# Issuing the compressed-branch transposes of the next head one unit earlier on TensorE

## The chip, the core and the metric

The kernel runs on one core of a Trainium2 chip. A core has engines that run their own instruction streams and meet through semaphores: TensorE (PE: matmuls, and PEld for its weight loads), VectorE (DVE), ScalarE (ACT), GpSimd (POOL), and SyncE (SP), which here only starts DMA transfers. The metric is the device time of the one launch, in microseconds; lower is better. The part that matters here is attention, where three engines pass small tiles to each other unit by unit.

## The reference

One decoder layer on 512 tokens of width 1024, in float32: an adaptive norm, a combined input projection, two groups of attention heads, an output projection, and a grouped mixture of 16 experts. The part around the change is the first head group, which has three branches over the same queries:

```
q_n = rms_norm(q_n, q_gain_n) * ATTN_SCALE
o_cmp, p_cmp = nsa_compressed(q_n, k_c, v_c, ...)     # 31 compressed keys, each from 32 tokens
o_slc = nsa_selected(q_n, k_sl, v_sl, p_cmp, ...)     # 8 blocks, all selected at this length
o_win = banded_attention(q_n, k_w, v_w, ..., 512)
o_nsa = g0 * o_cmp + g1 * o_slc + g2 * o_win
# nsa_compressed:
s = q @ kc.T - slope * dist;  s = where(valid, s, -1e30)
p = softmax(s) * row_valid;   o = p @ vc
```

The second group (SWA) is banded attention with window 128 and a learned sink per head.

## The kernel before

Heads are worked on in pairs, one head of each of the two key/value groups on 64 partitions each. There are GQ = 4 pairs t = 0 to 3 of the first group (NSA) and 4 of the second. A pair of the first group is cut into NU = 5 units j = 0 to 4, a pair of the second into 2; u counts all 28 units. Every unit goes through the same steps, and each engine has its own order, written out by hand:

- TensorE `scores(u)` (L1366): queries times keys into one of two pairs of PSUM banks (score).
- VectorE `masked(u)` (L969): adds the position term, takes the row extreme, writes `probs`; three buffers.
- ScalarE `exps(u)` (L585): exponentials with their sums.
- VectorE `weights(u)` (L989, L996, L1001): multiplies by gate over sum.
- TensorE `weighed_T(u)` (L1379): transposes the weighted probabilities, eight 128x128 tiles.
- ScalarE and VectorE `evac(u)` (L596, L1009): each copies one half to SBUF.
- TensorE `values(u)` (L1402): product with V, accumulated in PSUM over the five units of the pair. For j = 0 the accumulation starts with L1392, the product of the compressed branch, which needs `pcT`.

The compressed branch of pair t runs beside them: `cmp_scores` on TensorE (L1411), `cmp_masked` on VectorE (L1016 to L1018), `cmp_exp` on ScalarE (L601), `cmp_weights` on VectorE (L1022, L1023, L1025, L1026), which signals `c_w`; then `cmp_T` on TensorE (L1418), four transposes that wait for `c_w` and signal `c_t`; then `cmp_T` on ScalarE (L606), a copy to `pcT` that signals `c_T`. ScalarE runs its copy behind `out_T` of the pair before (L576, L577). VectorE makes the scores and weights of pair t + 1 in units 3 and 4 of pair t: in unit 4 in the order masked(u + 2), evac(u), weights(u + 1), cmp_weights(t + 1). TensorE is three units ahead with its scores: in unit u it issues scores(u + 3), which is the last thing it does in the unit.

A wait stops the whole instruction stream of its engine: what stands behind a waiting instruction on TensorE doesn't start. Four more pieces touch the order: `queries_T` (L1354), the transposed queries of the next pair, in unit 1; the preamble with scores(0) to scores(2) and cmp_T(0); and behind attention the output projection (L1454), the routing and the experts (L1524 to L1549). SyncE loads expert weights 0 when the last `values` is through (`a_pv`). The lines of the loop that the change touches:

```
                if 0 < t < GQ and j == 0:
                    cmp_T(t)
                if t < GQ - 1 and j == 1:
                    queries_T(t + 1)
```

Of the kernel before, what the change touches and what calls it, by code (L numbers as in the profile page):

```python
# [19 lines left out]
GQ = HN // KV  # L20
# [32 lines left out]
def decoder_layer(nc, x, c, w_router, ada_w, ada_b, norm1_g, norm2_g, w_in, w_out, nsa_q_gain, nsa_k_gain,  # L53
# [6 lines left out]
    with ctx:  # L60
# [283 lines left out]
        def unit_of(u):  # L344
            if u < GQ * NU:
                return u // NU, u % NU, NSA_UNITS[u % NU]
            i, j = (u - GQ * NU) // SU, (u - GQ * NU) % SU
            return GQ + i, j, SWA_UNITS[j]
# [4 lines left out]
        def slot_of(t):  # L353
            return t % 2 if t < GQ else SWA_SLOT[t - GQ]
# [438 lines left out]
        def _(dve):  # L793
# [107 lines left out]
            for n, (c0, r0, _) in enumerate(KSRC):  # L901
                nc.vector.tensor_tensor(khat[:, n, :, :].rearrange("p i (v d) -> p i v d", v=KV),
                                        proj[:, :, c0:c0 + KV * DH].rearrange("p i (v d) -> p i v d", v=KV),
                                        hrstd[:, :, r0:r0 + KV].unsqueeze(3).broadcast_to([P, TT, KV, DH]), ALU.mult).then_inc(s_khat, 1)
# [316 lines left out]
        def _(pe):  # L1221
# [124 lines left out]
            def queries_T(t):  # L1346
                pe.wait_ge(a_q, t + 1)
                Y = banks[6 + (t if t < GQ else GQ) % 2]
                if t > GQ:
                    pe.wait_ge(a_qT, t)  # L1350
                if GQ >= t >= 2:
                    pe.wait_ge(n_o, t - 1)
                for i in range(TT):
                    m = nc.tensor.transpose(Y[:, i * P:(i + 1) * P], qhat[t % 2][:, i, :], ident[:])  # L1354
                m.then_inc(a_qt, 1)

            def scores(u):
                t, j, segs = unit_of(u)
                if j == 0:
                    pe.wait_ge(a_qT, t + 1)  # L1360
                if u >= 2:
                    pe.wait_ge(a_m, u - 1)
                for q, r, off, w, k0 in segs:
                    for b in range(2):
                        half = slice(b * DH, (b + 1) * DH)
                        m = nc.tensor.matmul(banks[2 * (u % 2) + b][:, off:off + w], qT[half, slot_of(t), q * P:(q + 1) * P],  # L1366
                                             kT[half, r, k0:k0 + w], start=True, stop=True)
                m.then_inc(a_s, 1)

            def weighed_T(u):  # L1370
                t, j, segs = unit_of(u)
                pe.wait_ge(a_d, u + 1)
                if u >= 1:
                    pe.wait_ge(a_ev_a, u)
                    pe.wait_ge(a_ev_v, u)
                for q, r, off, w, k0 in segs:
                    for at0 in range(off, off + w, P):
                        for b in range(2):
                            m = nc.tensor.transpose(banks[4 + b][:, at0:at0 + P], probs[:, u % 3, b, at0:at0 + P], ident[:])  # L1379
                m.then_inc(a_t, 1)  # L1380

            def values(u):
                t, j, segs = unit_of(u)
                O = banks[6 + t % 2]
                if j == 0:
                    if t >= 2:
                        pe.wait_ge(n_o, min(t - 1, GQ))
                    if t > GQ + 1:
                        pe.wait_ge(w_o, t - GQ - 1)
                    if t < GQ:  # L1390
                        pe.wait_ge(c_T, t + 1)
                        nc.tensor.matmul(O, vcBD[0:2 * NK, :], pcT[0:2 * NK, :], start=True, stop=False, skip_group_check=True)  # L1392
                    else:
                        if t == GQ:
                            pe.wait_ge(a_qT, 2 * GQ)
                        nc.tensor.matmul(O, zeros_b[:, 0:P], zeros_b[:], start=True, stop=False, skip_group_check=True)
                pe.wait_ge(a_ev_a, u + 1)
                pe.wait_ge(a_ev_v, u + 1)
                for q, r, off, w, k0 in segs:
                    for n in range(w // P):  # L1400
                        for b in range(2):
                            m = nc.tensor.matmul(O[b * DH:(b + 1) * DH, q * P:(q + 1) * P],  # L1402
                                                 proj[:, k0 // P + n, V_COL[r] + b * DH:V_COL[r] + (b + 1) * DH],
                                                 probsT[:, u % 2, b, off + n * P:off + (n + 1) * P], start=False, stop=False,
                                                 skip_group_check=True)
                m.then_inc(a_pv, 1)

            def cmp_scores(t):
                pe.wait_ge(a_qT, t + 1)
                for i in range(TT):  # L1410
                    m = nc.tensor.matmul(banks[6 + t % 2][:, i * 2 * NK:(i + 1) * 2 * NK], qT[:, slot_of(t), i * P:(i + 1) * P], kcBD,  # L1411
                                         start=True, stop=True)
                m.then_inc(c_s, 1)

            def cmp_T(t):
                pe.wait_ge(c_w, t + 1)
                for i in range(TT):
                    m = nc.tensor.matmul(banks[6 + t % 2][0:2 * NK, i * P:(i + 1) * P], scm[:, i, :, :].rearrange("p b n -> p (b n)"),  # L1418
                                         ident[:], start=True, stop=True)
                m.then_inc(c_t, 1)  # L1420
# [8 lines left out]
            for u in range(N_UNITS):  # L1429
                t, j, segs = unit_of(u)  # L1430
                weighed_T(u)
                if u >= 1:
                    values(u - 1)
                if 0 < t < GQ and j == 0:
                    cmp_T(t)
                if t < GQ - 1 and j == 1:
                    queries_T(t + 1)
                if t == GQ - 1 and j >= 1:
                    queries_T(GQ + j - 1)
                if t < GQ - 1 and j == 2:  # L1440
                    cmp_scores(t + 1)
                if u + 3 < N_UNITS:
                    scores(u + 3)
            values(N_UNITS - 1)
# [157 lines left out]
```

## Time and profile before

| what | us |
| --- | --- |
| median of 3 runs | 766.3 (763.06 to 767.3) |
| profiled execution | 763.06 |
| its span | 761.3 |
| TensorE busy | 619.2 (81%) |
| VectorE busy | 325.2 (43%) |
| ScalarE busy | 253.6 (33%) |

A busy time says how long an engine had work in it, not whether that work set the end. Attention lies between about 197 and 324 us of the span; for a change there the timelines of the engines side by side say more than the shares of the whole span. An idle time with a releaser (`<-DVE pool_sb L1001`) says that the engine stood still until that instruction was done. In the profile `score` and `bank` are PSUM tiles; `pool_sb` is a large SBUF tile that holds, among much else, `probs`, `probsT`, `scm` and `pcT`.

### The profile page before, as it was taken

Reading aid. Unit: us, or ns where it says so; the run is one execution under the profiler, and the core shown is the slowest. Engines: PE = TensorE matmul, PEld = TensorE weight load, DVE = VectorE, ACT = ScalarE, POOL = GpSimd, SP = SyncE. Lnnn points to the kernel's source line nnn. Section 1 sums busy time; section 2 is a strip of 40 time slices with the busy share of each in tenths; the row PEclk is TensorE's granted clock in tenths of the full one; section 3 lists DMA queues with packets and bytes.
Section 4 is the critical chain, followed back from the end, with each engine's and each line's share of the span. In section 5 each row is a group of like instructions: output and inputs, shape, how many; then the busy total and the mean of one; then the engine's idle time right before and its main releaser. Section 6 shows DMA issues by size and latency. Waiting matters only on the chain.

```text
span 761.3 us, 15584 instructions
## 1 busy us (share of the span) xinstructions
PE 619.2 (81%) x6207; PEld 371.4 (49%) x6211; DVE 325.2 (43%) x925; ACT 253.6 (33%) x611; POOL 78.2 (10%) x118
## 2 busy tenths in 40 slices
PE   0898999967599998799972288989999999999940
PEld 0544474654366666554462154545555555555520
DVE  3714828242578999822445021222222222222215
ACT  4200200132357668711230142434433433443410
POOL 5001000034100000000001200101001101100122
PEclk9998999989689999999965599999999999999985
DMA  8970957070799000092081659999999999999228
GB/s 323 379 299 10 404 194 274 2 232 0 234 302 250 17 2 1 1 335 107 0 320 46 218 174 352 362 360 363 369 360 361 370 362 362 363 374 355 59 53 309
DMA packets 81388, 176.25 MB, mean 231 GB/s; under 512 B 9410, under 2 KB 26378, under 8 KB 79306
## 3 DMA queue, kind: packets, MB, share of 16 engines
q1 hardware_dynamic: 68592, 152.90, 57.5%
q0 software_dynamic: 8384, 13.97, 5.4%
q10 hardware_dynamic: 4380, 8.94, 3.7%
q8 instruction: 21, 0.34, 0.2%
q14 instruction: 11, 0.09, 0.0%
HBM read 155.02 MB, written 20.71 MB: 231 GB/s over the span
## 4 chain that ended last, share of the span: by engine, by line
PE 27%; DMA 23%; DVE 2%; issue 2%; POOL 2%; ACTq 0%; ACT 0%; POOLq 0%
DMA featT<-expert_rows 21%; PE score L1534 9%; PE score L1454 7%; PE score L1543 4%; PE bank L1524 4%; PE score L1494 2%; DMA pool_sb<-expert_rows,idx 1%; POOL expert_rows L768 1%; POOL pool_sb L788 1%; DMA expert_rows<-pool_sb,idx 1%; DMA expert_rows<-featT 1%; PE bank L1549 0%; ACTq L664 0%; PE bank L1486 0%; PE bank L1402 0%
## 5 line engine op out<-in xcount | busy, mean ns | idle before, releaser
L1534 PE MATMUL score<-pool_sb,featT 128*32 128x256 f32 x2688 | 161.4, 384 | 23.4 <-DMA featT<-expert_rows 14.7
L1534 PEld LDWEIGHTS score<-pool_sb,featT 128*32 128x32 f32 x2688 | 86.4, 110 | 84.4 <-DMA featT<-expert_rows 29.9
L1250 PE MATMUL bank<-pool_sb,featT 128*128 128x512 f32 (+2 forms) x256 | 89.3, 511 | 5.8 <-DVE featT L843 2.6
L1190 DVE TENSOR_TENSOR featT<-featT,score 128x128 f32<-128x128 f32 x42 | 12.1, 288 | 186.2 <-ACT featT L675 186.2
L1543 PE MATMUL score<-pool_sb,featT 128*32 128x256 f32 x1344 | 82.8, 387 | 0.4 <-ACT featT L680 0.4
L1250 PEld LDWEIGHTS bank<-pool_sb,featT 128*128 128x128 f32 x256 | 50.0, 196 | 43.5 <-issue 35.8
L669 ACT ACTIVATE featT<-bank,mod_col 128x32 f32<-128x32 f32 x129 | 39.3, 374 | 61.5 <-PE bank L1524 61.5
L776 POOL DMA_DIRECT2D expert_rows<-featT x42 | 29.1, 692 | 280.2 <-DVE featT L1186 266.5
L1180 DVE TENSOR_SCALAR featT<-bank,mod_col 128x32 f32<-128x32 f32 x215 | 51.0, 303 | 15.1 <-PE bank L1524 15.1
L1454 PE MATMUL score<-pool_sb,featT 128*128 128x512 f32 x128 | 55.6, 594 | 0.0
L675 ACT ACT_TABLE_LOAD x42 | 53.9, 1283 | 0.8
L1543 PEld LDWEIGHTS score<-pool_sb,featT 128*32 128x32 f32 x1344 | 39.9, 111 | 24.7 <-issue 1.4
L585 ACT ACTIVATE pool_sb<-pool_sb,nmax 128x128 f32<-128x128 f32 (+2 forms) x96 | 50.0, 526 | 4.5 <-DVE nmax L969 4.5
L675 ACT ACTIVATE featT<-score 128x128 f32<-128x128 f32 x42 | 11.6, 277 | 116.1 <-PE score L1534 116.1
L1524 PE MATMUL bank<-ident,featT 32*128 32x32 f32 x344 | 29.8, 226 | 19.6 <-DMA featT<-expert_rows 19.6
L1524 PEld LDWEIGHTS bank<-ident,featT 32*128 32x128 f32 x344 | 25.0, 139 | 37.0 <-DMA featT<-expert_rows 19.7
L1379 PE MATMUL bank<-ident,pool_sb 128*128 128x128 f32 x216 | 30.7, 286 | 14.2 <-DVE pool_sb L1001 14.0
L859 DVE SCALAR_TENSOR_TENSOR pool_sb<-pool_sb,cond 128x2048 f32<-128x2048 f32 x16 | 37.6, 2347 | 3.6 <-DMA pool_sb<-in_ada_w 2.6
L1454 PEld LDWEIGHTS score<-pool_sb,featT 128*128 128x128 f32 x128 | 24.0, 190 | 29.4 <-issue 28.9
L1379 PEld LDWEIGHTS bank<-ident,pool_sb 128*128 128x128 f32 x216 | 23.9, 144 | 29.1 <-DVE pool_sb L1001 27.4
L1366 PE MATMUL score<-pool_sb 64*128 64x256 f32 (+3 forms) x192 | 34.3, 475 | 0.9 <-ACT pool_sb L570 0.9
L1186 DVE TENSOR_TENSOR featT<-score,gate_part 128x256 f32<-128x256 f32 x42 | 17.8, 425 | 34.0 <-PE score L1543 34.0
(243 smaller groups left out, 688.0 us busy)
## 6 DMA issues: line engine op xcount, KB each, us to landing
pool_sb<-in_moe_w SPq DMA_DIRECT2D x48, 2048.0 KB, 21.2
pool_sb<-in_ada_w SPq DMA_DIRECT2D x16, 1024.0 KB, 7.4
expert_rows<-zeros_f SPq DMA_DIRECT2D x17, 512.0 KB, 6.2
featT<-expert_rows ACTq DMA_DIRECT2D x44, 128.0 KB, 5.5
expert_rows<-featT POOLq DMA_DIRECT2D x42, 128.0 KB, 7.1
pool_sb<-in_ada_w SPq DMA_DIRECT2D x8, 640.0 KB, 12.3
pool_sb<-in_w_out SPq DMA_DIRECT2D x4, 1024.0 KB, 16.7
pool_sb<-in_ada_w SPq DMA_DIRECT2D x8, 384.0 KB, 9.7
```

The costliest lines, as they stand in the source:

```text
L585: m = nc.scalar.activation(p, p, ACT.Exp, scale=-1.0, bias=nmax[:, u % 3, b, n:n + 1], accum_out=sums[:, u % 3, b, n:n + 1])
L669: m = nc.scalar.activation(xgT[:, 5 + k, :], banks[5][:, k * BT:(k + 1) * BT], ACT.Identity, scale=mod_col[:, 21 + k:22 + k], bias=mod_col ...
L675: nc.scalar.activation(silu, banks[0][:, 0:HB], ACT.Silu).then_inc(m_si, 1)
L859: nc.vector.scalar_tensor_tensor(out=acc[:, g % 2, :], in0=stage[:, n % 3, :], scalar=cond[:, k:k + 1], in1=acc[:, g % 2, :], op0=ALU.mult ...
L1180: m = nc.vector.tensor_scalar(xgT[:, k, :], banks[4][:, k * BT:(k + 1) * BT], mod_col[:, 16 + k:17 + k], mod_col[:, 24 + k:25 + k], ALU.mu ...
L1250: m = nc.tensor.matmul(pj_bank(g, i)[:, 0:n], featT[:, k, i * P:(i + 1) * P], w_stage[:, g % 3, k, 0:n], start=(k == 0), stop=(k == KD - 1))
L1366: m = nc.tensor.matmul(banks[2 * (u % 2) + b][:, off:off + w], qT[half, slot_of(t), q * P:(q + 1) * P], kT[half, r, k0:k0 + w], start=True ...
L1379: m = nc.tensor.transpose(banks[4 + b][:, at0:at0 + P], probs[:, u % 3, b, at0:at0 + P], ident[:])
L1454: m = nc.tensor.matmul(banks[2 * (j % 2) + g], featT[:, 4 * g + k, i * P:(i + 1) * P], w_out_sb[:, 4 * g + k, h], start=(k == 0), stop=(k ...
L1524: m = nc.tensor.transpose(banks[4 + k // 5][:, at0:at0 + BT], xg[:, k * P:(k + 1) * P], ident[0:BT, 0:BT])
L1534: mm = nc.tensor.matmul(banks[0][h * BT:(h + 1) * BT, 0:2 * HB], xgT[:, k, :], exp_w13[slot][:, :, k, h * HB:(h + 1) * HB], start=(k == 0) ...
L1543: mm = nc.tensor.matmul(banks[2][h * BT:(h + 1) * BT, 0:DN], hT[:, c * BT:(c + 1) * BT], exp_w2[slot][:, c, h * DN:(h + 1) * DN], start=(c ...
```

## The change

In the unit loop of TensorE the call of `cmp_T` for pair t leaves unit 0 of pair t, where it stood behind values(u - 1), and is made in unit 4 of pair t - 1, again behind values(u - 1) and ahead of scores(u + 3). This holds for pairs 1, 2 and 3; cmp_T(0) in the preamble stays where it is. Nothing else is changed.

```
@@ -1431,14 +1431,14 @@
                 weighed_T(u)
                 if u >= 1:
                     values(u - 1)
-                if 0 < t < GQ and j == 0:
-                    cmp_T(t)
                 if t < GQ - 1 and j == 1:
                     queries_T(t + 1)
                 if t == GQ - 1 and j >= 1:
                     queries_T(GQ + j - 1)
                 if t < GQ - 1 and j == 2:
                     cmp_scores(t + 1)
+                if t < GQ - 1 and j == 4:
+                    cmp_T(t + 1)
                 if u + 3 < N_UNITS:
                     scores(u + 3)
```

The instructions of TensorE from the values product in unit 4 of pair 0 on; names in brackets are the semaphores that an instruction waits for (`a_m`: masked, `a_d`: weights, `a_ev_a` and `a_ev_v`: the copies, `c_w`: cmp_weights). A minus is the order before, a plus the order after:

```order
 L1402 MATMUL bank<-pool_sb 64x128 [waits a_ev_v,a_ev_a]
 L1402 MATMUL bank<-pool_sb 64x128 x7
-L1366 MATMUL score<-pool_sb 128x128 [waits a_m]
-L1366 MATMUL score<-pool_sb 128x128
-L1366 MATMUL score<-pool_sb 128x384 x2
-L1379 MATMUL bank<-ident,pool_sb 128x128 [waits a_ev_v,a_ev_a,a_d]
-L1379 MATMUL bank<-ident,pool_sb 128x128 x7
-L1402 MATMUL bank<-pool_sb 64x128 [waits a_ev_v,a_ev_a]
-L1402 MATMUL bank<-pool_sb 64x128 x7
 L1418 MATMUL bank<-ident,pool_sb 64x128 [waits c_w]
 L1418 MATMUL bank<-ident,pool_sb 64x128 x3
+L1366 MATMUL score<-pool_sb 128x128 [waits a_m]
```

The four transposes L1418, with their wait for `c_w`, now stand in front of a scores group, a group of probability transposes and a values group which they stood behind.

VectorE's stream at the same place, the end of unit 4 and the start of unit 0 of the next pair, is the same before and after:

```order
L1001 TENSOR_SCALAR pool_sb<-pool_sb,fac 128x512 [waits a_chain]
L1022 TENSOR_REDUCE cfac<-pool_sb 128x8 [waits c_e]
L1023 RECIPROCAL cfac<-cfac 128x8 [waits a_chain]
L1025 TENSOR_TENSOR cfac<-cfac,gates 128x8 [waits a_chain]
L1026 TENSOR_TENSOR pool_sb<-pool_sb,cfac 128x256 [waits a_chain]
L969 ISA pool_sb,nmax<-score,pool_sb 128x128 [waits a_t,a_s]
```

L1026 signals `c_w`; the masking L969 right behind it waits for `a_s`, the scores group L1366 that TensorE now issues behind L1418.

## Rows read from the trace of the kernel before

**Rows 1.** The page: TensorE's busy tenths in 40 slices of the span.

```profile
PE   0898999967599998799972288989999999999940
```

**Rows 2.** One period; columns: length, busy PE, PEld, DVE, ACT, POOL, clock, DMA.

```profile
235.76:256.90 21.14, 19.31 (x175) 13.44 (x175) 19.12 (x72) 14.35 (x44) 0.00 (x0) 1.00 0.60 165
```

**Rows 3.** Waits of attention, 197 to 325 us: total, times, longest.

```profile
PE bank L1379 <- DVE pool_sb L1001: 14.0, 18, 1.6
DVE pool_sb L969 <- PE score L1366: 9.1, 8, 4.2
```

**Rows 4.** TensorE's timeline: start, length, instruction, idle time before it.

```profile
250.25 1.14 PE L1366 MATMUL score<-pool_sb 64*128 64x128 f32 x8
252.46 1.09 PE L1379 MATMUL bank<-ident,pool_sb 128*128 128x128 f32 x8 [1.07 <-DVE pool_sb L1001]
253.48 1.09 PE L1402 MATMUL bank<-pool_sb 128*64 128x128 f32 x16
254.40 1.04 PE L1418 MATMUL bank<-ident,pool_sb 128*64 128x128 f32 x8
255.37 1.14 PE L1366 MATMUL score<-pool_sb 64*128 64x128 f32 x8
256.90 1.09 PE L1379 MATMUL bank<-ident,pool_sb 128*128 128x128 f32 x8 [0.39 <-DVE pool_sb L1001]
...
260.58 1.13 PE L1366 MATMUL score<-pool_sb 64*128 64x256 f32 x8
```

**Rows 5.** VectorE: all four L1026, then its timeline at the same boundary.

```profile
L1026 DVE TENSOR_TENSOR pool_sb<-pool_sb,cfac x4: 424/425/426, 208.3 to 274.4; 128x256 f32<-128x256 f32 x4
...
253.21 0.43 DVE L1026 TENSOR_TENSOR pool_sb<-pool_sb,cfac 128x256 f32<-128x256 f32 x1
253.55 0.28 DVE L969 CUSTOM_DVE_ANT_0 pool_sb<-score,pool_sb 128x128 f32<-128x128 f32 x1
...
254.97 0.69 DVE L1009 COPY pool_sb<-bank 128x512 f32<-128x512 f32 x1
...
259.34 0.17 DVE L989 RECIPROCAL fac<-sums 128x4 f32<-128x4 f32 x1
...
261.77 0.42 DVE L969 CUSTOM_DVE_ANT_0 pool_sb<-score,pool_sb 128x256 f32<-128x256 f32 x1 [0.89 <-PE score L1366]
```

**Rows 6.** ScalarE's timeline at the same boundary.

```profile
253.59 0.60 ACT L596 ACTIVATE pool_sb<-bank 128x512 f32<-128x512 f32 x1 [1.42 <-PE bank L1379]
254.62 0.60 ACT L576 ACTIVATE pool_sb<-bank 128x512 f32<-128x512 f32 x1 [0.44 <-PE bank L1402]
...
258.13 0.58 ACT L596 ACTIVATE pool_sb<-bank 128x512 f32<-128x512 f32 x1
```

**Rows 7.** TensorE's timeline in the first pair, at the slower granted clock.

```profile
208.77 1.97 PE L1418 MATMUL bank<-ident,pool_sb 128*64 128x128 f32 x8 [2.12 <-DVE pool_sb L1026]
210.66 1.97 PE L1379 MATMUL bank<-ident,pool_sb 128*128 128x128 f32 x8
212.56 2.08 PE L1366 MATMUL score<-pool_sb 64*128 64x128 f32 x8
```

**Rows 8.** TensorE's timeline: instructions behind three longer idle times.

```profile
175.58 14.03 PE L1325 MATMUL bank<-pool_sb 128*62 128x256 f32 x64 [2.88 <-DVE pool_sb L914]
195.62 0.31 PE L1343 MATMUL bank<-ident,pool_sb 31*128 31x31 f32 x1 [3.47 <-DVE pool_sb L930]
459.56 0.64 PE L1534 MATMUL score<-pool_sb,featT 128*32 128x256 f32 x8 [1.60 <-DMA featT<-expert_rows]
```

**Rows 9.** Stretches behind these idle times, columns as in rows 2.

```profile
175.58:178.00 2.42, 2.42 (x11) 1.54 (x12) 0.00 (x0) 0.00 (x0) 2.42 (x1) 1.00 0.00 0
195.62:208.77 13.15, 9.09 (x30) 4.82 (x30) 7.38 (x22) 6.08 (x14) 0.72 (x2) 0.50 0.97 324
208.77:214.60 5.83, 5.83 (x24) 4.06 (x24) 3.18 (x14) 2.52 (x9) 0.00 (x0) 0.50 1.04 346
459.56:463.90 4.34, 4.34 (x48) 2.18 (x48) 1.47 (x6) 1.19 (x4) 0.00 (x0) 0.62 1.05 387
```

More of the change, by code:

```diff
@@ L1433, in _ @@
                     values(u - 1)
-                if 0 < t < GQ and j == 0:
-                    cmp_T(t)
                 if t < GQ - 1 and j == 1:
@@ L1441, in _ @@
                     cmp_scores(t + 1)
+                if t < GQ - 1 and j == 4:
+                    cmp_T(t + 1)
                 if u + 3 < N_UNITS:
```

## The prediction

> **What bounds the kernel now.** I read the page first, then the busy time of one period, the waits, and the timelines of TensorE, VectorE and ScalarE around one boundary between two heads. On the page TensorE has 81% of the span, but in the part that the change touches (about 197 to 323 us) it is not full everywhere: slices 12 to 17 of its row read 9, 9, 9, 9, 8, 7 [rows 1]. From one second unit of a head to the next, 21.14 us, TensorE is busy 19.31 and VectorE 19.12 [rows 2]. Neither alone is the bound. They hand over to each other: TensorE waits 14.0 us in 18 pieces for the weighted probabilities of VectorE (L1001), and VectorE waits 9.1 us in 8 pieces for scores of TensorE (L1366) [rows 3].
>
> Where in a head does which engine set the pace? Around the boundary into head pair 2, TensorE finishes the values product before 250.25, does the scores of the next unit 2 (250.25), then idles 1.07 us until VectorE releases the transposes of unit 0 at 252.46; then values, the moved transposes L1418 (254.40 to 255.37), scores of unit 3 (255.37), and again 0.39 us idle before unit 1 at 256.90 [rows 4]. VectorE is without a gap there: the last row of compressed weights (L1026) starts at 253.21 and the next masking of scores at 253.55 [rows 5]. So at the boundary VectorE is the bound and TensorE has slack. Behind unit 1 it is the other way round: VectorE idles 0.89 us before 261.77, waiting for the scores issued at 260.58 [rows 4, 5]. What lies behind attention starts from its last unit: output projection, routing, and the expert weights, whose loads SyncE holds until the last values product. I therefore count a delay inside attention in full at the end.
>
> **The change, part by part.** No instruction is added or removed. On TensorE the four transposes of cmp_T for heads 1, 2 and 3 go from unit 0 of their head to unit 4 of the head before: ahead of one scores group, one group of probability transposes and one values group. cmp_T(0) stays. The other queues are unchanged, and no DMA moves.
>
> *What it takes away:* four transposes between values and scores at unit 0, 255.37 - 254.40 = 0.97 us, three times [rows 4]. Worth nothing: there TensorE idles 0.39 us behind them already, released by VectorE. The earlier copy on ScalarE is worth nothing either: the product that needs it (L1392) is not waiting in the rows; it starts when the transposes ahead of it are through.
>
> *What it adds:* cmp_T waits for L1026, and now the scores of the next head's unit 2 are queued behind that wait. L1026 runs four times for 0.42 us [rows 5]. At this boundary it ends at 253.21 + 0.43 = 253.64; from the end of such a row to the first row on TensorE it takes 0.05 (208.3 + 0.42 = 208.72 against 208.77 [rows 5, 7]), so cmp_T starts at 253.69. Before it, TensorE is free from 250.25 on (less a few hundredths in which the values product ends): it now stands idle for 3.4 us in one piece. Then 0.97 for cmp_T: the scores start at 254.66 instead of 250.25. From the start of a scores group to VectorE's first masking it takes 261.77 - 260.58 = 1.19 us [rows 4, 5], so masking starts at 255.85 instead of 253.55: **2.3 us later**. This is the wait that replaces nothing: VectorE, the bound here, had its scores ready three microseconds early and now has none.
>
> Does it shorten again? VectorE runs masking, copy and weights without a gap from 253.55 until it releases unit 1 at 256.90, 3.35 us; after: 255.85 + 3.35 = 259.20, against 256.90, again 2.3. TensorE in that time does scores 1.06, transposes 1.02, values 1.0 and the scores of unit 3 (about 1.1) from 254.66: through at 258.84, in front of 259.20. The transposed probabilities of unit 0 reach VectorE at 255.72 + 1.13 = 256.85 (the 1.13 is 253.59 - 252.46 [rows 4, 6]), and VectorE wants them at 255.85 + 1.42 = 257.27 (1.42 is 254.97 - 253.55 [rows 5]); in time by 0.4. ScalarE comes closest: its block behind the values product took from 254.62 to the end of the exponentials at about 258.13 [rows 6], 3.5 us; the values product now ends so that the block starts at 255.72 + 1.02 + 1.14 = 257.88 (1.14 is 254.62 - 253.48 [rows 4, 6]), ending at 261.4, and VectorE wants the exponentials at 259.34 + 2.3 = 261.64 [rows 5]. In time by 0.2. From unit 1 on everything hangs on the released unit 1, the 0.89 us of VectorE included, because the scores that it waits for also come 2.3 us later. Nothing is given back. The same three boundaries: 3 x 2.3 = 6.9 us.
>
> *The clock.* The second term is the TensorE clock after the new gap. The period has a granted clock of 1.00, the 2.4 GHz level, with gaps of 1.07 us at most at its boundary [rows 2, 4]. A piece of 3.4 us is new here. The nearest rows on either side: behind a wait of 2.88 us at 175.58 the clock was 1.00; behind one of 3.47 us at 195.62 it was 0.50, the 1.2 GHz level, for 13 us and more [rows 8, 9]. Behind a short 1.60 us at 459.56, with small matmuls around it, it was 0.62 [rows 8, 9]. 3.4 is nearest to the one that fell. But the length of a gap does not decide alone, as the short one that fell and the longer one that held show, so I don't take all three: I take two of three.
>
> What does a slow resumption cost? Rows at the slow level: cmp_T 210.66 - 208.77 = 1.89 (0.97 fast), transposes 212.56 - 210.66 = 1.90 (1.02 fast), scores 214.60 - 212.56 = 2.04 (1.06 fast) [rows 7, 4]. Both groups that release VectorE are directly on the path: slow throughout, +0.92 and about +1.0. The next transposes add 0.88, of which 0.4 is covered. If the clock returns in the middle of the scores, the price is about 1.7; if it stays slow through values and the scores of unit 3 it is 1.9 + 0.5 + about 0.5 = 2.9; a clock that returns at once or is lost only late costs near 0. Upper bound: TensorE at half speed for the whole of the next packed stretch, as the 13 us of the first head, some 4.6. I take the middle of 1.7 and 2.9, **2.3 us for each slow resumption**; 2 x 2.3 = 4.6.
>
> The Trainium skill has a rule against this change: TensorE: Matmul & The Clock Gate, "HAM oscillation — how this bites in real kernels", says that idle waits between bursts of matmuls throttle the clock again, so that each burst starts cold. By that rule alone all three resumptions would be slow. The rows bear it out only in part: the 2.88 us wait kept its clock. The sum by the rule would be 3 x 2.3 + 3 x 2.3 = 13.8, by the row that held 6.9.
>
> **Sum.** 6.9 + 4.6 = 11.5 us. The profiled execution took 763.06 us (span 761.3 and 1.8 around it), the lowest of the three; it would become 774.6. The median of the runs is 766.3, and the forecast is made for the median: 766.3 + 11.5 = **777.8 us**.
>
> **Rivals.**
> 1. *The clock holds in all three gaps.* For it: 2.88 us kept it, and every gap in the heads so far. Against it: 3.47 us lost it. Time 766.3 + 6.9 = 773.2. Chance 0.16.
> 2. *All three resume slow* (what the skill's rule would give, here worked out from the rows above): 6.9 + 3 x 2.3 = 13.8, 780.1; with 2.9 each 781.9. For it: three gaps of equal length. Against it: the kept 2.88 us. With the forecast it is one family (at least one slow resumption), 0.70 together, of which 0.25 is this one.
> 3. *The delay is absorbed.* VectorE has 0.89 us of idle time behind unit 1 and a shorter one behind unit 2; if both soaked up the delay, 2.3 - 1.5 = 0.8 per boundary would be left, 2.4 in all: 768.7, which is within 0.5%. Against it: those idle times wait for TensorE, whose chain starts from the same late unit 1. Chance 0.06.
> 4. *Slow for long:* three resumptions at 4.6 and the 6.9: 766.3 + 20.7 = 787.0. For it: the first head, slow although TensorE was full from 208.77 to 214.60 [rows 7, 9]. Chance 0.06.
> 5. *Faster.* If L1026 were done before TensorE reaches cmp_T at 250.3, the moved transposes would fill idle time and unit 0 would be shorter by 0.97: at best 3 x 0.97 = 2.9 us, 763.4. The point from which it decides is VectorE 3.4 us earlier than the rows show; the price of VectorE's own work would have to drop for that. With TensorE clearly bound at the boundary it would be real. Chance 0.02; a gain under 3.8 us would then count as no change.
>
> **How the numbers follow.** The range has to hold 8 in 10. Low end: rival 1 less 1.5 for spread between runs (they lie 763.06 to 767.3): 771.5. High end: rival 2 with its higher price, 781.9, and 2.6 for the same spread and for a longer slow stretch: 784.5. Left out are rivals 3, 4, 5 and a little of each edge. A measurement of this kernel can tell about 0.5%, 3.8 us, from no change: 6.9 alone is beyond that. Slower: 0.70 + 0.16 + 0.06 = 0.92. Same: 0.07 (rival 3 and most of 5). Faster by more than that: 0.01.
>
> **What would show it.** In the changed profile TensorE's row at L1418 must carry an idle time of about 3.4 us, three times, with L1026 as releaser; VectorE's first masking behind L1026 must show a wait of about 2.3 us for scores L1366, three times, which it doesn't have now; the 1.07 and 0.39 us before unit 0 and unit 1 must be gone or smaller; the period must be 23.4 us where the clock holds and 25 to 26 where it falls, with a granted clock well under 1.00 behind L1418. ScalarE's exponentials must not become what VectorE waits for. Everything behind 324 us must be shifted as a block. I'm wrong if cmp_T finds its data ready, if VectorE shows no new wait, or if the part behind attention gives the time back.

## The result, and the profile after

| | before | after |
| --- | --- | --- |
| median | 766.66 us (763.06 to 767.3, 4 runs) | 777.19 us (776.22 to 777.72, 4 runs) |
| profiled execution | 763.06 us | 775.59 us |
| its span | 761.3 us | 773.9 us |

The kernel became slower: the ratio is 1.0147, 95% interval 1.0118 to 1.0176; 10.5 us between the medians, 12.5 between the two profiled executions. Here and below a ratio with its interval compares the undisturbed (fast) runs and is not the quotient of the medians, which is 1.0137 here. The forecast was 777.8 us. The page of the kernel after: span, TensorE's busy tenths, and its granted clock in tenths, each in 40 slices.

```profile
span 773.9 us, 15587 instructions
PE   0898999967689888889975088989999999999940
...
PEclk9998999989598999999985589999999999999985
```

Slices 12 to 17 of TensorE's row read 8, 9, 8, 8, 8, 8 where they read 9, 9, 9, 9, 8, 7 [rows 1], and the thirteenth (232 to 251 us), in the middle of attention, has a clock of 0.8, where it had 0.9. More can't be seen at this scale. The stretches of the kernel after, each from the transposes of unit 1 in one pair to those in the next, with the columns of [rows 2]:

```profile
214.98:240.95 25.97, 22.24 (x176) 15.40 (x175) 19.41 (x72) 12.38 (x37) 0.00 (x0) 0.87 1.03 252
240.95:265.64 24.69, 20.96 (x176) 14.29 (x174) 19.09 (x72) 14.31 (x44) 0.00 (x0) 0.93 0.33 100
265.64:290.65 25.01, 20.93 (x177) 14.55 (x175) 19.85 (x73) 14.64 (x45) 0.00 (x0) 0.93 0.00 1
```

The three periods before were 21.16, 21.14 and 21.18 us [rows 2 has the second]. They are now longer by 4.81, 3.55 and 3.83: 12.2 of the 12.6 us between the spans. VectorE's busy time is the same (19.09 against 19.12 in the middle one). TensorE's rose by 1.65 although it has the same instructions, and the clock is 0.93 instead of 1.00: some of them ran slowly. TensorE's timeline at the boundary into pair 2, the place of [rows 4]:

```profile
254.41 1.09 PE L1402 MATMUL bank<-pool_sb 128*64 128x128 f32 x16
258.87 1.40 PE L1418 MATMUL bank<-ident,pool_sb 128*64 128x128 f32 x8 [3.36 <-DVE pool_sb L1026]
260.20 2.08 PE L1366 MATMUL score<-pool_sb 64*128 64x128 f32 x8
262.21 1.41 PE L1379 MATMUL bank<-ident,pool_sb 128*128 128x128 f32 x8
263.55 1.09 PE L1402 MATMUL bank<-pool_sb 128*64 128x128 f32 x16
264.57 1.14 PE L1366 MATMUL score<-pool_sb 64*128 64x128 f32 x8
265.64 1.09 PE L1379 MATMUL bank<-ident,pool_sb 128*128 128x128 f32 x8
```

This is the whole case in seven lines. After the values product TensorE idles 3.36 us in one piece, with L1026 as releaser. The scores L1366, which need nothing from L1026, start at 260.20, behind the four transposes. They take 2.08 us where they took 1.14 [rows 4], and the two groups around them 1.40 and 1.41. Over that stretch the granted clock is 0.59, so mostly the 1.2 GHz level, where before it was 1.00, 2.4 GHz, throughout:

```profile
258.87:263.00 4.13, 4.13 (x20) 2.72 (x21) 0.67 (x3) 0.00 (x0) 0.00 (x0) 0.59 0.03 6
```

The idle 1.07 and 0.39 us of before are gone here (at the third boundary 0.24 us is left). VectorE at the same boundary, beside [rows 5]:

```profile
258.39 0.42 DVE L1026 TENSOR_TENSOR pool_sb<-pool_sb,cfac 128x256 f32<-128x256 f32 x1
262.33 0.29 DVE L969 CUSTOM_DVE_ANT_0 pool_sb<-score,pool_sb 128x128 f32<-128x128 f32 x1 [3.52 <-PE score L1366]
...
268.34 0.18 DVE L989 RECIPROCAL fac<-sums 128x4 f32<-128x4 f32 x1 [0.18 <-ACT pool_sb L585]
```

It used to go from L1026 straight on to L969. Now it stands 3.52 us for the scores (4.08 and 3.73 at the other two boundaries). The waits of attention, 197 to 340 us (total, times, longest), beside [rows 3]:

```profile
DVE pool_sb L969 <- PE score L1366: 19.9, 11, 4.2
PE bank L1418 <- DVE pool_sb L1026: 12.2, 4, 3.4
PE bank L1379 <- DVE pool_sb L1001: 10.0, 13, 1.6
```

VectorE's waits for scores went from 9.1 to 19.9 us. Behind attention nothing was given back: from the first output-projection matmul (L1454) to the end of the span it was 761.3 - 324.25 = 437.05 us, and is 773.9 - 336.82 = 437.08. That they agree this closely is luck: in the twelve profiles of this case this part takes 434.7 to 442.3 us, whatever was changed in attention.

### The profile page after: what moved, and what is told of

Same layout as the page of the kernel before. It is cut to its first block, busy times and chain, and to the rows that moved or that the text cites. A ratio compares the mean times of both kernels' runs of the same rounds, so it can differ in the third digit from the quotient of the medians.

```text
span 773.9 us, 15587 instructions
## 1 busy us (share of the span) xinstructions
PE 627.6 (81%) x6210; PEld 375.8 (49%) x6211; DVE 325.6 (42%) x925; ACT 253.9 (33%) x611; POOL 79.6 (10%) x118
## 4 chain that ended last, share of the span: by engine, by line
PE 27%; DMA 23%; DVE 2%; issue 2%; POOL 2%; ACTq 0%; ACT 0%; POOLq 0%
DMA featT<-expert_rows 21%; PE score L1534 9%; PE score L1454 7%; PE score L1543 4%; PE bank L1524 4%; PE score L1494 2%; DMA pool_sb<-expert_rows,idx 1%; POOL expert_rows L768 1%; POOL pool_sb L788 1%; DMA expert_rows<-pool_sb,idx 1%; DMA expert_rows<-featT 1%; PE bank L1549 0%; ACTq L664 0%; PE bank L1486 0%; PE bank L1402 0%
## 5 line engine op out<-in xcount | busy, mean ns | idle before, releaser
L1534 PE MATMUL score<-pool_sb,featT 128*32 128x256 f32 x2688 | 162.6, 386 | 21.0 <-DMA featT<-expert_rows 12.2
L1454 PE MATMUL score<-pool_sb,featT 128*128 128x512 f32 x128 | 55.6, 594 | 0.0
L1379 PE MATMUL bank<-ident,pool_sb 128*128 128x128 f32 x216 | 31.8, 293 | 10.1 <-DVE pool_sb L1001 10.0
L1454 PEld LDWEIGHTS score<-pool_sb,featT 128*128 128x128 f32 x128 | 24.0, 190 | 29.4 <-issue 28.9
L1366 PE MATMUL score<-pool_sb 64*128 64x256 f32 (+3 forms) x192 | 36.8, 504 | 0.9 <-ACT pool_sb L570 0.9
L1379 PEld LDWEIGHTS bank<-ident,pool_sb 128*128 128x128 f32 x216 | 24.9, 148 | 25.9 <-DVE pool_sb L1001 21.4
L969 DVE CUSTOM_DVE_ANT_0 pool_sb<-score,pool_sb 128x128 f32<-128x128 f32 (+2 forms) x64 | 27.9, 486 | 20.0 <-PE score L1366 19.9
```

The lines of the kernel that those rows point to most:

```text
L1454: m = nc.tensor.matmul(banks[2 * (j % 2) + g], featT[:, 4 * g + k, i * P:(i + 1) * P], w_out_sb[:, 4 * g + k, h], start=(k == 0), stop=(k ...
L1534: mm = nc.tensor.matmul(banks[0][h * BT:(h + 1) * BT, 0:2 * HB], xgT[:, k, :], exp_w13[slot][:, :, k, h * HB:(h + 1) * HB], start=(k == 0) ...
```

## The experiments

What was to be told apart: the wait itself, the moved transposes, the order of the scores behind them, and the clock. Runs of one kernel spread widely here: the kernel before from 762.78 to 771.17 us in one comparison, b1_scores_first from 761.38 to 772.13. A period inside attention repeats to 0.1 us from profile to profile as long as the clock holds. So the periods of the profiles decide, and the times are given beside them.

**The change for one pair only** (pair 2; pairs 1 and 3 stay in unit 0):

```diff
--- after
+                if t == 1 and j == 0:
+                    cmp_T(1)
+                if t == 3 and j == 0:
+                    cmp_T(3)
-                if t < GQ - 1 and j == 4:
-                    cmp_T(t + 1)
+                if t == 1 and j == 4:
+                    cmp_T(2)
```

> The change for pair 2 alone; cmp_T of pairs 1 and 3 stays in unit 0. Theory: one boundary's price, 2.3 us and 1.3 to 2.5 for the clock: 3.6 to 4.8 us slower than before, and the other two boundaries as in the profile of before (21.1 us periods). Rival (a fixed price once the order is broken, or absorption by the next pair): over 6 or under 2 us.

Measured: 770.83 us against 765.43, ratio 1.0045 (1.0011 to 1.0079). Its three periods:

```profile
218.12:239.31 21.19, 19.41 (x177) 13.53 (x175) 19.08 (x72) 13.66 (x41) 0.00 (x0) 0.99 1.03 261
239.31:265.02 25.71, 21.97 (x174) 15.25 (x175) 19.31 (x72) 13.02 (x40) 0.00 (x0) 0.87 0.50 136
265.02:286.21 21.19, 19.31 (x176) 13.43 (x174) 19.72 (x73) 15.57 (x48) 0.00 (x0) 1.00 0.00 1
```

Only the boundary with the moved transposes pays, 25.71 - 21.14 = 4.57 us, and the next pair absorbs none of it. The price is per boundary. But it is not a fixed one: the change itself paid 3.55 us at this same boundary, behind the same gap (3.36 us there, 3.37 here). The difference is in the slow stretch: here L1418 took 1.97 us and the transposes L1379 behind the scores 1.85, there 1.40 and 1.41. So the clock's part of the price differs by 1 us between two profiles, and every size given for it below is that of one profile.

**The wait without the move:**

```diff
--- before
+                if t < GQ - 1 and j == 4:
+                    pe.wait_ge(c_w, t + 2)
                 if u + 3 < N_UNITS:
                     scores(u + 3)
```

> The kernel before with only the wait for c_w put at the new place in unit 4, ahead of scores(u + 3); the four transposes of cmp_T stay in unit 0. Theory: the gap is the same 3.4 us, the scores start at 253.69 instead of 254.66, masking 1.3 us late; the transposes, now on TensorE's path at unit 0, give 0.6 of it back: 1.9 us per boundary, 5.7 us, and the slow clock behind the gap again 1.3 to 2 us each: 9.5 to 11 us slower than before, as the change within 1.5 us. Rival (the moved transposes are what costs): less than 3 us.

Measured: 778.48 us against 765.43, ratio 1.0154 (1.0088 to 1.022). Two of its periods, and the release in TensorE's timeline:

```profile
218.91:244.73 25.82, 22.08 (x177) 15.58 (x175) 19.81 (x72) 13.39 (x41) 0.00 (x0) 0.87 1.03 252
244.73:269.28 24.55, 20.81 (x177) 14.53 (x175) 19.34 (x71) 14.18 (x43) 0.00 (x0) 0.93 0.34 102
...
236.85 2.08 PE L1366 MATMUL score<-pool_sb 64*128 64x128 f32 x8 [3.37 <-DVE pool_sb L1026]
```

With 24.65 for the third that is 4.66, 3.41 and 3.47 us over before, 11.5 in all, against 12.2 of the change. A wait with no work behind it does nearly all the damage. Whether the remaining 0.7 us is the price of the transposes isn't shown, since the clock's part alone can differ by more. My 9.5 to 11 us was a little low, by the periods and more so by the times. The rival, under 3 us, falls.

**The gap filled with work.** Extra matmuls ahead of cmp_T give TensorE something to do while it would wait. There are eleven of them here, and seven and three in the two kernels that follow:

```diff
--- after
                 if t < GQ - 1 and j == 4:
+                    pe.wait_ge(a_m, u + 2)
+                    for n in range(11):
+                        nc.tensor.matmul(banks[2 * ((u + 3) % 2)][:, 0:256], qT[:, slot_of(t), 0:P], qT[:, slot_of(t), 0:256],
+                                         start=True, stop=True)
                     cmp_T(t + 1)
```

> The changed kernel with eleven extra matmuls (128x128 by 128x256, results overwritten by the next scores) between the values product and cmp_T in unit 4, three times: TensorE has work in most of the 3.4 us gap, cmp_T still waits for L1026. Nothing else differs. Theory (each boundary pays 2.3 us for scores queued behind the wait and 1.3 to 2.5 us for a slow clock behind the gap): the clock stays at 1.00, cmp_T and scores take 1.04 and 1.14 us again, VectorE's wait before masking is 2.3 us, and the kernel is 6.9 us slower than before instead of 10.5. Rival 1 (the whole loss is order; slow matmuls are hidden behind VectorE): about 10.5 to 12 us slower, as the change. Rival 2 (the loss is all clock, the wait costs nothing): no slower than before within 1 us.

Measured: 779.64 us against 765.43, ratio 1.017 (1.0105 to 1.0235). This missed, because I filled too much. In its profile the eleven take from 252.67 to 257.62:

```profile
252.67 5.02 PE L1443 MATMUL score<-pool_sb 128*128 128x256 f32 x22
257.62 1.09 PE L1418 MATMUL bank<-ident,pool_sb 128*64 128x128 f32 x8
...
238.19:263.13 24.94, 24.33 (x196) 17.51 (x196) 19.17 (x72) 14.31 (x44) 0.00 (x0) 1.00 0.34 106
```

The clock held at 1.00 and L1418 took 1.09, but it started 6.99 us behind the last transposes of unit 4 (250.63) where the change has 258.87 - 253.39 = 5.48. Of the 24.94 us, 1.51 are my own overfill, which leaves 23.43. That was argued, so it was run again with seven:

> As a1_fill, with seven extra matmuls instead of eleven per boundary. The eleven took 4.95 us (0.45 each) and held cmp_T back 1.5 us beyond the release by L1026; seven take 3.15 us and end 0.2 us ahead of it. Theory: the clock stays at 1.00 and the wait alone is left: period 21.14 + 2.3 = 23.4 us, three times, 6.9 us over the kernel before and 3.6 to 5.3 us under the change. Rival (the price is order alone, the slow clock is hidden): periods of 24.7 to 26 us as in the change.

Measured: 773.38 us against 766.1, ratio 1.0113 (1.0063 to 1.0163). Periods, TensorE and VectorE at the second boundary:

```profile
217.44:240.95 23.51, 22.76 (x190) 16.07 (x189) 19.16 (x72) 12.70 (x38) 0.00 (x0) 1.00 1.03 255
240.95:264.39 23.44, 22.68 (x189) 15.99 (x189) 19.17 (x72) 14.30 (x44) 0.00 (x0) 1.00 0.45 128
264.39:287.93 23.54, 22.68 (x189) 15.99 (x189) 19.77 (x73) 14.30 (x44) 0.00 (x0) 1.00 0.00 1
...
258.87 1.09 PE L1418 MATMUL bank<-ident,pool_sb 128*64 128x128 f32 x8 [0.15 <-DVE pool_sb L1026]
259.89 1.14 PE L1366 MATMUL score<-pool_sb 64*128 64x128 f32 x8
...
261.08 0.29 DVE L969 CUSTOM_DVE_ANT_0 pool_sb<-score,pool_sb 128x128 f32<-128x128 f32 x1 [2.26 <-PE score L1366]
```

This separates the two terms. With the clock held, the order costs 2.35, 2.30 and 2.36 us, 7.0 in all. What the change has above that, 25.97 - 23.51, 24.69 - 23.44 and 25.01 - 23.54, is the clock: 2.46, 1.25 and 1.47, 5.2 us. By adding useless work attention got 5.2 us shorter than with the change. The times alone would not show it: the two intervals, 1.0118 to 1.0176 and 1.0063 to 1.0163, overlap. The rival (order alone) falls, and so does the one that calls it all clock.

How much idle time is too much? The same with three matmuls:

> The changed kernel with three extra matmuls ahead of cmp_T in each of the three gaps: 1.35 us of work, about 2.0 us of idle time left in one piece. The wait's own price stays at 2.3 us per boundary. What is asked is whether 2.0 us of idle time still loses the clock. By the kernel before (gaps of 1.9 and 2.3 us at 1.00, one of 1.6 at 0.62) I expect it to hold in at least two of three: periods of 23.4 us there, and 24.5 or more where it is lost.

Measured: 775.39 us, one run. Its second boundary, and the period around it:

```profile
259.72 1.09 PE L1418 MATMUL bank<-ident,pool_sb 128*64 128x128 f32 x8 [1.87 <-DVE pool_sb L1026]
...
241.80:265.23 23.43, 20.95 (x180) 14.47 (x181) 19.16 (x72) 14.29 (x44) 0.00 (x0) 1.00 0.44 127
```

Idle pieces of 1.88, 1.87 and 1.87 us kept the clock, three of three, with periods of 23.54, 23.43 and 23.53. Its one time is higher than its periods explain. Most of that lies behind attention: from L1454 to the end it takes 438.8 us, a5_fill7 435.2, both within the range given above.

**The same unit, behind the scores:**

```diff
--- after
-                if t < GQ - 1 and j == 4:
-                    cmp_T(t + 1)
                 if u + 3 < N_UNITS:
                     scores(u + 3)
+                if t < GQ - 1 and j == 4:
+                    cmp_T(t + 1)
```

> The changed kernel with cmp_T still in unit 4, but behind scores(u + 3) instead of ahead of it. Theory: VectorE's scores are on time, its wait before masking behind L1026 is gone. The probability transposes of unit 0 now start behind cmp_T, at 253.69 + 0.97 = 254.66 in the time scale of the kernel before instead of 252.46, so VectorE's copy of them, wanted at 254.97, gets them at 255.8: 0.8 us per boundary, 2.5 us in all if the clock holds. The gap is about 2.4 us (from 251.3 to 253.69), between one of 2.31 that held the clock and one of 2.65 that lost it; if it is lost each time, about 1 us more per boundary, 5.5 us in all. Rival (it is the wait of TensorE as such that costs, whatever stands behind it): 2.3 us and more per boundary, 7 us or more.

Measured: 770.4 us against 765.43, ratio 1.0055 (1.002 to 1.0091). Two periods, TensorE at the two boundaries, and VectorE at the first:

```profile
215.96:238.10 22.14, 19.47 (x176) 13.49 (x174) 19.22 (x72) 12.39 (x37) 0.00 (x0) 1.00 1.03 258
238.10:261.78 23.68, 21.01 (x176) 14.81 (x175) 19.80 (x72) 14.31 (x44) 0.00 (x0) 0.93 0.50 139
...
233.97 1.09 PE L1418 MATMUL bank<-ident,pool_sb 128*64 128x128 f32 x8 [2.30 <-DVE pool_sb L1026]
...
256.03 1.09 PE L1418 MATMUL bank<-ident,pool_sb 128*64 128x128 f32 x8 [2.30 <-DVE pool_sb L1026]
257.05 1.93 PE L1379 MATMUL bank<-ident,pool_sb 128*128 128x128 f32 x8
...
236.12 0.69 DVE L1009 COPY pool_sb<-bank 128x512 f32<-128x512 f32 x1 [0.83 <-PE bank L1379]
```

The wait for scores is gone, as the order theory says, and what is late next is the copy L1009, by 0.83 us: the first boundary costs 0.98 where I had worked out 0.8. The gap of 2.30 us held the clock once and lost it twice (23.68, and 23.76 for the third), which adds 1.56 and 1.60 where I expected 1. The rival, 2.3 us and more whatever stands behind the wait, falls at the first boundary. The other two cost 2.54 and 2.58 us, but only with the clock's part.

**Scores in front of every helper.** If what hurts is anything ahead of scores that VectorE needs, the kernel before has the same fault in small: queries_T and cmp_scores stand ahead of scores.

```diff
--- before
+                if u + 3 < N_UNITS:
+                    scores(u + 3)
                 if 0 < t < GQ and j == 0:
                     cmp_T(t)
...
-                if u + 3 < N_UNITS:
-                    scores(u + 3)
```

> The kernel before with scores(u + 3) issued right behind values(u - 1) in every unit, ahead of cmp_T, queries_T and cmp_scores. If what counts is that nothing stands in front of the scores VectorE waits for, VectorE's 0.89 us in unit 1 shrinks by 0.58 (queries_T) and its 0.61 us in unit 2 by up to the same; but the copies of the transposed probabilities then come late by 0.8 us, so I expect 20.8 to 21.1 us per period against 21.14, 0 to 1.5 us faster in all. Rival (the order of the helpers doesn't matter at all): the same period to 0.05 us.

Measured: 766.89 us against 766.1, ratio 1.0025 (0.9994 to 1.0055), no difference that can be told. Periods 21.13, 21.17 and 21.81: the expected gain is not there. The same with cmp_scores one unit later, behind the scores there:

> As b1_scores_first, with cmp_scores(t + 1) moved from unit 2 to unit 3, behind scores(u + 3), where TensorE idles 0.37 us before the next transposes. Theory: TensorE's stretch from unit 1 to the scores of the next pair, which sets the pace there, is 1.03 us shorter; some of it is lost again as VectorE's masking of the compressed scores waits about 0.8 us: 20.3 to 21.0 us per period, 0.5 to 3 us faster in all. Rival (VectorE's row of work is the bound and nothing is won): 21.1 us or more.

Measured: 770.65 us against 766.1, ratio 1.0049 (1.0023 to 1.0075). Periods 22.28, 22.24 and 22.20, over 1 us longer, where I had expected them shorter. Both expectations failed on one step: I had watched two engines and not the third. In both kernels VectorE now waits 1.12 us for exponentials, where it waited for none before. b2 has a second wait of its own: VectorE stands 0.97 us in two of its periods, and 0.29 in the third, until the later cmp_scores are through (L1016), which I had put at 0.8. ScalarE and VectorE of b1_scores_first:

```profile
260.99 0.69 ACT L570 ACTIVATE pool_sb<-bank,gain_col 128x512 f32<-128x512 f32 x1 [2.02 <-PE bank L1354]
...
263.67 0.18 DVE L989 RECIPROCAL fac<-sums 128x4 f32<-128x4 f32 x1 [1.12 <-ACT pool_sb L585]
```

On ScalarE the copy L570 waits for queries_T, and the exponentials that VectorE needs are queued behind that copy. The copy waited 1.99 us in the kernel before too; what is new is that queries_T comes later, so that the copy starts 4.86 us into the period (260.99 - 256.13) where it started 3.79 (260.69 - 256.90). It is the mechanism of the change again, on another engine. Two edits follow: the exponentials first on ScalarE,

```diff
--- b1_scores_first, ScalarE
-                if t < GQ - 1 and j == 1:
-                    queries_T(t + 1)
-                if t == GQ - 1 and j >= 1:
-                    queries_T(GQ + j - 1)
...
                 if u + 2 < N_UNITS:
                     exps(u + 2)
+                if t < GQ - 1 and j == 1:
+                    queries_T(t + 1)
+                if t == GQ - 1 and j >= 1:
+                    queries_T(GQ + j - 1)
```

> b1_scores_first with one more edit, on ScalarE: the exponentials of unit u + 2 are issued ahead of the copy of the transposed queries (L570), not behind it. In b1 and b2 that copy waited 2.0 us for its transposes with the exponentials behind it, and VectorE stood 1.12 us for them (L989). Theory (the same head-of-line wait, on another engine): that 1.12 us is gone, the period is 0.2 to 0.6 us under b1's 21.13 to 21.81, 0.5 to 2 us faster than before in all. Rival (ScalarE had nothing to do with it): b1's periods again.

and, on top of it, `cmp_scores(t + 1)` in unit 3 of TensorE's loop, ahead of `scores(u + 3)`:

> b3_exps_first, with cmp_scores(t + 1) moved from unit 2 to unit 3, ahead of scores(u + 3) there. TensorE's stretch from unit 1 to the transposes of unit 3 is 1.03 us shorter than in b3, and in unit 3 it has idle time in front of the transposes of unit 4. Theory: VectorE is without a gap for nearly the whole period: 19.9 to 20.3 us instead of 21.14, three times, and a little at the first pair: 3 to 4 us faster than before. Rival (cmp_scores late makes VectorE's cmp_masked wait, as in b2): 20.7 us or more per period, 1 us or less in all.

Measured: with the first edit 765.06 us against 765.01, ratio 0.9997 (0.9969 to 1.0026); with both 762.96, ratio 0.9952 (0.9921 to 0.9984). Periods: 20.62, 20.62 and 20.60 with the first; with both

```profile
218.72:238.75 20.03, 19.42 (x177) 13.54 (x175) 19.10 (x72) 13.03 (x38) 0.00 (x0) 0.99 1.03 263
238.75:258.71 19.96, 19.30 (x174) 13.42 (x174) 19.15 (x72) 14.60 (x44) 0.00 (x0) 1.00 0.71 187
258.71:279.31 20.60, 19.30 (x174) 13.43 (x175) 19.75 (x73) 14.62 (x44) 0.00 (x0) 1.00 0.00 1
```

The first edit takes 1.6 us out of the three periods, as expected, too little to show in the times. VectorE's wait for exponentials is gone. Both together take 1.13, 1.18 and 0.58, 2.9 us, where I had expected 3 to 4, and that kernel is the fastest of the case: 0.5% under the kernel before, its interval clear of 1. VectorE is now busy 19.15 of the 19.96 us in the second period. The third misses the 19.9 to 20.3 us; VectorE has one instruction more there (L1035, 0.69 us), which the kernel before hid in an idle time. That this is the reason was not tested.

## Why the prediction was right, and where it wasn't

- **VectorE is the bound at the boundary, and the moved wait takes its scores away.** Right, mechanism and size. The gap is 3.36 us for 3.4; cmp_T starts 0.06 us behind the end of L1026 for 0.05; with the clock held VectorE waits 2.26 us and the period grows by 2.30 to 2.36 for 2.3. The sum of 6.9 us is 7.0 in a5_fill7.
- **What the change takes away is worth nothing.** Right in the main: the wait alone costs 11.5 of the 12.2 us.
- **Nothing is given back.** Right: one changed boundary costs 4.57 us and its neighbours nothing, and the part behind attention takes as long as before within the spread of the profiles.
- **ScalarE stays in time by 0.2 us.** Right with the clock held: a5_fill7 has no such wait. In the change it failed at two boundaries of three: VectorE waits 0.33 and 0.18 us for its exponentials, which I had named as something that must not happen. With the slower clock the margin was used up. I count no cost for it, because TensorE runs on without a gap through units 1 and 2 at both; that is read from the timeline and not tested.
- **The clock: two of three at 2.3 us, 4.6.** The term was nearly right (5.2) by luck, by two errors that cancel. The count was wrong: 3.4 us lost the clock at all three boundaries, and in the two kernels with the same gap, four more times. The price was wrong too: 2.46, 1.25 and 1.47 us, mean 1.7, where I took the middle of 1.7 and 2.9. The first is inside those bounds. The other two are below them, because there the clock was low for less of the work: at the second boundary it still read 1.00 from 258.87 to 259.30, with L1418 already running, and fell to 0.50 behind that, so L1418 took 1.40 us and not 1.97; at the third it came back within the scores, 1.73 us and not 2.08. I had named values near zero for that and left them out of the middle. I had also missed a row: in the kernel before TensorE idles 2.65 us ahead of 65.64, and the clock behind it is 0.50. With it, the 2.88 us that held is the exception among the waits near 3 us, which speaks rather for three of three.
- **The total.** 11.5 us was forecast; 12.5 between the profiled executions, 10.5 between the medians. That the median came within 0.6 us of 777.8 is partly luck: the kernel before alone spreads by 4 us in this comparison and by 8.4 in a later one. (The low end of the range is 773.2 - 1.5 = 771.7 by its own sum, not 771.5; nothing hangs on it.)
- **Among the rivals** it was the second that happened, all three resuming slowly, with 0.25; its 13.8 us was too much, by the price of a resumption. The first (the clock holds, 773.2) is what a5_fill7 builds on purpose: 773.38.

The Trainium skill, in TensorE: Matmul & The Clock Gate, "HAM oscillation — how this bites in real kernels", has each burst start cold behind an idle wait; the waits of its example are some 3 to 5 us. The gap of this change, 3.36 or 3.37 us, lost the clock seven times of seven, but two of the seven bursts did not start cold: their first groups took 1.40 and 1.46 us, between the fast and the slow time. Pieces under those of the example went both ways: 1.87 and 1.88 us lost nothing in three, 2.30 us lost the clock in two of three. The same page, "Step-by-step: what each phase is for", says that TensorE may load weights ahead but keeps its matmuls in program order. The trace agrees: scores with all their inputs ready started only behind cmp_T, 260.20 against 258.87.

## What to carry to other kernels

In a stream that runs in order, price a moved instruction by its wait and not by its work: look up when its input is ready, and who needs the instructions that then stand behind it. Before work for later is moved ahead of work that another engine is about to need, look for the engine without a gap at that place; if it is the one that would be kept waiting, whatever makes it late is paid in full each time (2.3 us here, for a move of 0.97 us of work). A TensorE wait that grows into one long piece has a second price, the clock behind it, and an order that frees one engine has to be followed through all three, since the same fault may sit in the next queue.

## What the runs showed that I had not expected

- Useless work made attention shorter: seven matmuls put into each gap took 5.2 us out of it against the change, and three matmuls, which left 1.87 us idle, did as well.
- Gaps of equal length don't have equal effects: 2.30 us kept the clock once and lost it twice. It can also go after work has resumed: behind the second of those gaps L1418 still took 1.09 us, and the transposes behind it 1.93.
- 0.45 us for each filler matmul of 128x128 by 128x256 in float32 with the full 128 rows, where I had assumed 0.27 from scores groups on 64 rows. That is why the first filler overshot.
